# Differential attention on TensorE: value products over both query tiles of a kind, head copies on ScalarE

## The reference, cut to what matters

```python
def attend(q_blk, k, v):
    s = jnp.einsum('bqhmd,bkhmd->bhmqk', q_blk, k).astype(f32) * scale
    p = jax.nn.softmax(s, axis=-1)
    p = p[:, :, 0] - lam * p[:, :, 1]
    return jnp.einsum('bhqk,bkhe->bqhe', p.astype(v.dtype), v)
```

## Time and profile before

| what | us |
|---|---|
| median of 3 runs | 2132.37 |
| the three runs | 2131.66, 2132.37, 2137.76 |
| the profiled execution's own time | 2135.11 |
| its span in the trace | 2132.7 |
| TensorE busy | 1932.3 (91%) |
| VectorE busy | 816.6 (38%) |
| ScalarE busy | 296.2 (14%) |
| first attention, scores of job 0 to normalising of job 31 | 251.2 to 321.4 |

### The profile page before, as it was taken

How to read it: one execution, slowest core, us unless ns; L and a number is a source line. 1 busy time by engine, 2 the same in 40 slices (tenths; PEclk the granted TensorE clock), 3 DMA queues, 4 the chain that set the end, 5 groups by cost and what they waited for, 6 DMA issues and landing times.

```text
span 2132.7 us, 23354 instructions
## 1 busy us (share of the span) xinstructions
PE 1932.3 (91%) x9268; PEld 1385.8 (65%) x9268; DVE 816.6 (38%) x1504; ACT 296.2 (14%) x710; POOL 68.3 (3%) x122
## 2 busy tenths in 40 slices
PE   7999999999999999998999999999999886666765
PEld 5586465788888885684888888886887532212221
DVE  6597696667778224128211102125113200000001
ACT  2200281210110001107100000014001100000000
POOL 1011000000000011000000000000000000000000
PEclk9999999999999999999999999999999788888887
DMA  9454303345343144320344534441464799999996
GB/s 362 159 211 173 118 1 125 103 154 181 139 176 140 55 153 100 138 82 18 118 148 152 178 125 144 150 141 57 149 264 191 291 420 422 421 422 422 421 422 279
DMA packets 86020, 422.72 MB, mean 198 GB/s; under 512 B 9841, under 2 KB 9969, under 8 KB 60913
## 3 DMA queue, kind: packets, MB, share of 16 engines
q1 hardware_dynamic: 70416, 364.10, 44.8%
q0 software_dynamic: 15520, 57.45, 7.7%
HBM read 420.47 MB, written 2.95 MB: 199 GB/s over the span
## 4 chain that ended last, share of the span: by engine, by line
PE 74%; DMA 17%; DVE 6%; issue 1%; ACT 1%; SPq 1%; DVEq 0%; ACTq 0%
PE ps L701 28%; DMA ring<-in_up 9%; PE ps L723 7%; PE ps L940 7%; DMA ring<-in_gate 5%; PE ps L836 4%; PE ps L1300 3%; PE ps L745 3%; PE ps L755 3%; PE ps L785 3%; DMA ring<-in_down 2%; PE ps L776 2%; PE ps L1033 2%; PE ps L1051 2%; PE ps L1075 2%; DVE small L2029 1%
## 5 line engine op out<-in xcount | busy, mean ns | idle before, releaser
L701 PE MATMUL ps<-xn,ring 128*128 128x256 f32 (+1 forms) x1376 | 308.2, 385 | 3.0 <-ACT xn L1412 1.7
L701 PEld LDWEIGHTS ps<-xn,ring 128*128 128x128 f32 x1376 | 260.5, 190 | 49.0 <-issue 10.4
L701 PE MATMUL ps<-big,ring 128*128 128x256 f32 x736 | 162.2, 382 | 11.2 <-DMA ring<-in_memkv 9.7
L701 PEld LDWEIGHTS ps<-big,ring 128*128 128x128 f32 x736 | 140.4, 191 | 31.9 <-DMA ring<-in_memkv 10.0
L701 PE MATMUL ps<-aux,ring 128*128 128x257 f32 x704 | 153.4, 380 | 0.0
L701 PEld LDWEIGHTS ps<-aux,ring 128*128 128x128 f32 x704 | 133.6, 190 | 19.1 <-issue 0.4
L1300 PE MATMUL ps<-ring,aux 128*32 128x512 f32 x624 | 92.3, 720 | 58.8 <-DMA ring<-in_up 48.2
L2307 DVE TENSOR_TENSOR work<-work,ps 128x512 f32<-128x512 f32 x8 | 8.3, 1043 | 352.4 <-PE ps L1300 352.4
L940 PE MATMUL ps<-ring,xn 128*128 128x512 f32 x256 | 113.9, 601 | 5.5 <-ACT xn L1416 4.0
L1793 DVE SCALAR_TENSOR_TENSOR aux<-aux,scond 128x1024 f32<-128x1024 f32 x84 | 103.0, 1278 | 4.1 <-DMA aux<-in_ada 4.1
L1300 PEld LDWEIGHTS ps<-ring,aux 128*32 128x32 f32 x624 | 21.3, 121 | 126.8 <-issue 126.8
(11 more groups left out here) (345 smaller groups left out, 2796.5 us busy)
## 6 DMA issues: line engine op xcount, KB each, us to landing
ring<-in_gu SPq DMA_DIRECT2D x88, 512.0 KB, 3.4
ring<-in_up SPq DMA_DIRECT2D x44, 1024.0 KB, 25.3
aux<-in_ada POOLq DMA_DIRECT2D x80, 512.0 KB, 4.9
ring<-in_gate SPq DMA_DIRECT2D x34, 1024.0 KB, 25.0
ring<-in_wqkv SPq DMA_DIRECT2D x48, 512.0 KB, 4.7
ring<-in_down SPq DMA_DIRECT2D x32, 704.0 KB, 4.2
ring<-in_win SPq DMA_DIRECT2D x44, 512.0 KB, 3.2
xn<-in_gate SPq DMA_DIRECT2D x14, 1024.0 KB, 19.5
```

Source lines behind the costliest of these rows:

```text
L701: mm = pe.matmul(ps[:, bank(s, c), 0:T], ring[:, slot(s.u0, j), k * P:(k + 1) * P], rhs(kk), start=kk == 0, stop=kk == nk - 1)
```

## The change

The job order in a head becomes q = 0, 1, 2, 3, so S S B B. Both tiles of a kind write their transposed probabilities into one buffer, interleaved per block of keys (`pair_probs`: block k holds 256 columns, 128 of each tile). The context pairs have two such buffers, by head, the latent pairs one; `freed` is the count of `s_pv` for which the copy waits before it overwrites. The value products are made only behind the second tile of a pair, each with 256 columns, 2 for the context pair and 4 for the latent pair, and raise `s_pv` by 2. ScalarE copies the finished head out of its bank (`head_out`), ahead of its squares; VectorE's `outs` does nothing for these jobs.

```diff
--- before.py
+++ after.py
@@ -266,6 +266,11 @@
 
         E = work[:, 0:3072].rearrange("p (b c n) -> p b c n", b=3, c=2)
         PT = work[:, 3072:5120].rearrange("p (b n) -> p b n", b=4)
+
+        def pair_probs(h, late):
+
+            at = work[:, 3584:4608] if late else work[:, 3072 + 1536 * (h % 2):3584 + 1536 * (h % 2)]
+            return at.rearrange("p (k t) -> p k t", t=2 * P)
 
         def pair_block(pair, p, g):
 
@@ -441,16 +446,19 @@
 
         def da_jobs():
             for h in range(8):
-                for q in (0, 2, 1, 3):
-                    n = CTX if q < 2 else TOK
+                for q in range(4):
+                    n, late = (CTX if q < 2 else TOK), q // 2
+                    blocks = n // P
+                    at = pair_probs(h, late)
                     yield dict(
                         n=n, da=True, sums=first_sums[:, 4 * h + q:4 * h + q + 1],
                         scores=[[(qk[64 * c:64 * c + 64, h, q * P:q * P + P], qk[64 * c:64 * c + 64, 8 + h, 0:n], 0, n)]
                                 for c in range(2)],
-                        groups=[[(None, k) for k in range(n // P)]],
-                        pv=[[(0, P, q * P, vv[:, k, h * P:h * P + P], k * P, P, k == 0, k == n // P - 1)
-                             for k in range(n // P)]],
-                        first=q == 0, evac=xn[:, h, :] if q == 3 else None, out=(0, P, TOK))
+                        groups=[[(None, k) for k in range(blocks)]],
+                        turned=at[:, :, (q % 2) * P:(q % 2 + 1) * P], freed=4 * h if late else 4 * h - 6,
+                        pv=[[(0, P, late * CTX, vv[:, k, h * P:h * P + P], at[:, k, :], 256, k == 0, k == blocks - 1)
+                             for k in range(blocks)]] if q % 2 else [],
+                        first=q == 1, evac=xn[:, h, :] if q == 3 else None, out=(0, P, TOK))
 
         def na_jobs():
             for c in range(HEADS // 2):
@@ -1073,8 +1081,9 @@
                         pe.wait_ge(s_ptsb, G + 1)
                         for o, m, c, v, r, w, first, last in mms:
                             mm = pe.matmul(ps[o:o + m, 2 + J["o"] % 2, c:c + w], v,
-                                           r if "pair" in J else PT[:, G % 4, r:r + w], start=first, stop=last)
-                        mm.then_inc(s_pv, 2 if "pair" in J else 1)
+                                           r if "pair" in J or J["da"] else PT[:, G % 4, r:r + w], start=first,
+                                           stop=last)
+                        mm.then_inc(s_pv, 2 if "pair" in J or J["da"] else 1)
 
                 for i in range(a, b + BEHIND):
                     if i < b:
@@ -1493,6 +1502,11 @@
                                         asum[:, 2 * bf + p:2 * bf + p + 1])
                 mm.then_inc(s_exp, 1)
 
+            def head_out(j):
+                J = jobs[j]
+                act.wait_ge(s_pv, groups_before(j + 1))
+                act.activation(J["evac"], ps[:, 2 + J["o"] % 2, 0:TOK], ACT.Copy).then_inc(s_osb, 1)
+
             def head_squares(o):
                 squares(("suba", "subb")[o // 4], o % 4)
 
@@ -1506,6 +1520,12 @@
                         act.wait_ge(s_pv, J["g0"] - 2 * J["tile"] - 4)
                         act.activation(pair_block(J["pair"], J["tile"], g),
                                        ps[:, G % 2, :].rearrange("p (e n) -> p e n", e=2), ACT.Copy).then_inc(s_ptsb, 1)
+                        continue
+                    if J["da"]:
+                        if J["freed"] > 0:
+                            act.wait_ge(s_pv, J["freed"])
+                        act.activation(J["turned"], ps[:, G % 2, 0:w].rearrange("p (k t) -> p k t", t=P),
+                                       ACT.Copy).then_inc(s_ptsb, 1)
                         continue
                     if G >= 4:
                         act.wait_ge(s_pv, G - 3)
@@ -1522,10 +1542,12 @@
                         exps(i)
                     done = i - BEHIND - 1
                     if name == "da" and done >= a and jobs[done]["evac"] is not None:
+                        head_out(done)
                         head_squares(jobs[done]["o"])
                 if name == "da":
                     for j in range(b + 2 - BEHIND - 1, b):
                         if jobs[j]["evac"] is not None:
+                            head_out(j)
                             head_squares(jobs[j]["o"])
 
             squares("nmem")
@@ -2048,7 +2070,7 @@
 
             def outs(j):
                 J = jobs[j]
-                if J["evac"] is None:
+                if J["evac"] is None or J["da"]:
                     return
                 dve.wait_ge(s_pv, groups_before(j + 1))
                 src = ps[:, 2 + J["o"] % 2, 0:J["out"][2]]
```

## The result

| | before | changed |
|---|---|---|
| median, us | 2133.07 (9 runs) | 2138.55 (9 runs) |
| lowest to highest | 2130.29 to 2137.76 | 2136.80 to 2140.37 |
| ratio | | 1.0026, 95% interval 1.0018 to 1.0035 |
| span of the profiled execution | 2132.7 | 2136.3 |

A forecast was written before the change was run, and what follows sets the result against it. It took a ring of waits through TensorE and VectorE, 8.55 us per head, to bound the first attention. Steady and last heads +4.8, first head -0.4, tail -0.1 gave +4.3 on 2132.37, so 2136.7 us, range 2131 to 2141.

The forecast's parts named there:

- The ring: First attention, one head: a TensorE-VectorE ring of waits, 8.55 us, holding the head copy (0.60) and value products (1.53).
- The copy gives nothing: First attention: taking the 0.60 us head copy off VectorE gains nothing, since VectorE then waits for scores behind value bursts.
- A 256-column record at 0.217: TensorE's value products: each 256-column record costs 0.217 us, so a head's values fall from 3.06 to 2.61.
- The half loops: Steady head in the new order: two loops from maximum to maximum, 4.90 and 4.39 us, 9.29 together for 8.55.
- The last head and the tail: End of the first attention: last head 8.56 us; from its last normalising to the first diagonal, -0.1 us.
- The first head: Start of the first attention: normalising of job 3 ends at 261.5 against 261.86, -0.4 us.
- rival B: First attention: TensorE's idling lowers its clock to 1.2 GHz, 5.3 us per such head, one giving 2142 us; chance 0.10.
- Handed through whole: Behind the first attention: TensorE is the bound, so the stage's whole delay reaches the total, +4.3 us.
- C: Behind the first attention: later waits absorb the longer stage, or its start gains more; 2132.4 us; chance 0.10.
- A: First attention: VectorE's work decides and the order costs nothing, so faster, 2126.0 to 2127.6 us; chance 0.12.
- D: Value products: 256 columns save nothing, a record stays at 0.248 us, loops of 9.66, 2138.9 us; chance 0.10.

The follow-up runs named there:

- After_dve_copy: Changed kernel with the head copy back on VectorE; 9.46 us per head, median 2138.18 us, ratio 1.0029 to the kernel before.
- act_copy_only: Kernel before with only the head copy moved from VectorE to ScalarE; 8.25 us per head, median 2128.83 us, ratio 0.9985.
- act_copy_again: Second run of the kernel before with only the head copy moved to ScalarE; 8.24 us per head, median 2128.99 us, ratio 0.9986.
- pairs_alternating: Changed kernel in the old job order S B S B, two probability buffers per kind; 9.19 us per head, median 2133.99 us, ratio 1.0010.
- order_and_copy: Kernel before with order S S B B and head copy on ScalarE, 128-column products behind each job; 8.64 us per head, 2134.98 us, ratio 1.0009.
- split_values: Changed kernel with order S B B S, products ahead of turns, latent ones split, VectorE copy, part of latent sums left out; 2130.29 us, ratio 0.9992.

## Why the prediction was right

It said 2136.7 with 2131 to 2141; measured 2138.55. The direction, the size and the cause held. That the total came so near is partly luck: the stage grew by 6.65 where the terms sum to 4.3, and the medians show 5.5. The terms, in its order:

**The ring.** Right. After_dve_copy shows it from one side (a copy more or less on VectorE changes nothing at 9.46), act_copy_only from the other (in the old ring the copy counts, by 0.30).

**The copy gives nothing.** Right in the changed kernel. But the prediction didn't see that it is the good half of the change: alone it gives 0.3 per head. The new layout of the probabilities, which no row priced, cost nothing as assumed: their copies take 0.58 to 0.60 for a B job and 0.38 for an S job, 0.60 and 0.38 before.

**A 256-column record at 0.217.** The sum's mis-sized term. The record of the earlier trace rows came from a stream of 16 such products; behind a turn the bursts measured 1.82 for 8 and 0.96 for 4, 2.78 per head for 2.61. 9.29 + 0.17 = 9.46 is the head that was measured. Pairing saved 3.06 - 2.78 = 0.28 per head and not 0.45, and two thirds of that is the fixed part of each burst (fewer, longer bursts: 0.19), not the width, which gave 0.09.

**The half loops.** Predicted 4.90 and 4.39, measured 4.97 and 4.49. Right in kind: VectorE's two waits before its maxima, 0.66 and 1.24, were named as about 0.6 and 1.2. The claim that the order did it was too narrow. With the copy on ScalarE throughout, the ladder of measured heads is 8.24 (act_copy_only), 8.64 with the order, 9.55 with the grouping too, 9.46 with the width: +0.40, +0.91, -0.09. Grouping and width together in the old order, 9.19, cost 0.95 by themselves; so either the order with the grouping or the grouping in the old order is enough to lengthen the head.

**The last head and the tail.** Predicted 8.56 and -0.1; measured 328.30 - 319.69 = 8.61, and 4.76 for 4.79 from there to the first diagonal. Right.

**The first head.** Predicted -0.4, measured +0.8: TensorE's clock stood at 1.2 GHz until past 258 us, not 255. That is a part of rival B that the forecast's own term left out. How much of the 1.2 it explains is open; that it can be so much is shown by act_copy_only and act_copy_again, whose first heads are 9.48 at the full clock and 10.86 at the low one. The last job's normalising ended at 328.30, 2.6 later than the 325.7 forecast. In the steady heads the clock stayed at 1.00, as forecast.

**Handed through whole.** The stage is 6.65 longer, the median 5.5; the interval of the ratio, 3.8 to 7.5 us, holds both. Absorption in a later wait (C) isn't seen. Of the twelve comparisons with before, ten have a median that lies 1.0 to 2.9 us lower than the stage alone would give, whether their stage is longer (pairs_alternating, +5.1 and +2.2) or shorter (act_copy_only, -3.0 and -4.0); order_and_copy lies 1.6 and split_values 2.4 higher. A later wait that absorbs a delay would shrink both kinds toward zero. An offset of the one trace of before would move both alike; that it is this isn't shown.

**The rivals.** A fell: the two half loops came out at 9.46 and not under 8.0, and even without grouping act_copy_only stopped at 8.25. B didn't come within the steady heads, where the granted clock was 1.00. D, that pairing saves nothing, was the nearest to the truth of the products' price, and half of its extra came.

## What to carry to other kernels

When engines take turns in a hand-written order, ask of every moved or merged piece which ring of waits it falls into, before counting what it saves: the same products, with the same copy, take 9.46 per head behind the second job of a pair in the order S S B B, 9.19 in S B S B and 8.70 in S B B S. An idle stretch on an engine that ends with another engine's work is a warning that relieving it may give little: VectorE waited 0.31 for scores before and gave back half of the 0.60 it was relieved of; with 1.9 us of such waits it gave back nothing. Make the relief first and alone (here the copy on ScalarE, -0.15%), and look at which engine's lines then carry the chain. The price of a product taken from a long stream isn't its price in a short burst: take the time from the burst's start to the next instruction's start.

## What the runs showed that was not expected

- Small bursts have a price of their own on TensorE. 4 records of 128 columns hold the next instruction back 0.54, 8 of them 0.99, 16 of them 1.88, so about 0.11 each and some 0.1 per burst; 4 and 8 records of 256 columns 0.96 and 1.82, 0.215 each and again 0.1 per burst.
- A copy can be free on both of two engines that are some 80% busy: on VectorE and on ScalarE the head took 9.46.
- Stretches at 1.2 GHz of a few us fall on different places from one trace to the next (at 256, 326 or 392 us), also of one and the same kernel: act_copy_only has none at the stage's start, act_copy_again has one from 253 to 259 us. TensorE had been idle shortly before: 1.88 us ahead of the first scores, 2.16 us up to 391.50 in the changed kernel. In single traces they moved later marks by 2 to 5 us, as much as the change itself.
